# A transformer layer with sparse attention: first transfers reordered, two heads' compressed probabilities in one transpose, `p` split later

## The reference, cut to what matters

```
q, k_c, v_c, k_s, v_s, k_w, v_w, gate = split(rms_norm(x) @ w_in)
k_c, v_c = compress(k_c), compress(v_c)      # 15 blocks of 32 tokens, stride 16; silu(blk @ w1) @ w2
pc = masked_softmax(q @ k_c.T * scale)       # 15 columns: the compressed branch
ps = masked_softmax(q @ k_s.T * scale)       # all 256 tokens are selected here: causal
pw = masked_softmax(q @ k_w.T * scale)       # the window is 512: causal as well
o = gate0 * (pc @ v_c) + gate1 * (ps @ v_s) + gate2 * (pw @ v_w)
h = x + o @ w_out
```

## Time and profile before

| | us |
|---|---|
| median of three runs | 1208.03 (1207.96 to 1209.53) |
| profiled execution, own time | 1209.89 |
| its span | 1207.8 |
| TensorE busy | 1196.9 |
| VectorE busy | 729.1 |
| ScalarE busy | 590.7 |

### The profile page before, as it was taken

The page is one execution under the profiler, slowest core; times in us unless marked ns, Lnnn a source line. Parts: engine busy times, 40 slices in busy tenths (PEclk is TensorE's granted clock), DMA queues, the critical chain, the costliest instruction groups (busy, mean ns, idle before and its releaser), DMA issues.

```text
span 1207.8 us, 15258 instructions
## 1 busy us (share of the span) xinstructions
PE 1196.9 (99%) x5502; PEld 993.3 (82%) x5502; DVE 729.1 (60%) x956; ACT 590.7 (49%) x812; POOL 71.5 (6%) x63
## 2 busy tenths in 40 slices
PE   8999999999999999999999999999999999999998
PEld 7787788888888888888888888888888888888886
DVE  5676646777767647554465464555655457476554
ACT  6654444666656544443344443444433445455442
POOL 1000000000000002100011100011100012000000
PEclk9999999999999999999999999999999999999999
DMA  9776564333348766865567765577665676785661
GB/s 353 251 228 211 186 195 139 104 123 105 105 144 266 223 222 217 253 224 193 188 215 244 240 215 194 189 237 242 220 217 191 208 245 214 248 266 195 212 208 51
DMA packets 107134, 247.02 MB, mean 205 GB/s; under 512 B 9408, under 2 KB 52160, under 8 KB 107072
## 3 DMA queue, kind: packets, MB, share of 16 engines
q1 hardware_dynamic: 106784, 245.98, 62.4%
q10 hardware_dynamic: 288, 0.27, 0.1%
HBM read 232.58 MB, written 13.63 MB: 204 GB/s over the span
## 4 chain that ended last, share of the span: by engine, by line
PE 92%; DVE 3%; ACT 2%; DMA 2%; issue 1%; SPq 0%; ACTq 0%; DVEq 0%
PE acc L1413 85%; DMA w_raw<-in_nsa_w_in_units_dram 2%; PE sc L1554 2%; DVE w_split L936 1%; PE tr L1471 1%; ACT w_split L595 1%; ACT s L693 1%; PE sc L1519 0%; PE sc L1460 0%; PE tr L1460 0%; PE tr L1605 0%; PE tr L1606 0%; PE acc L1443 0%; ACT junk_act L645 0%; PE tr L1583 0%
## 5 line engine op out<-in xcount | busy, mean ns | idle before, releaser
L936 DVE TENSOR_TENSOR w_split<-w_raw,w_split 128x1024 fp32r<-128x1024 f32 x411 | 509.3, 1249 | 384.2 <-ACT w_split L595 383.7
L595 ACT ACTIVATE w_split<-w_raw 128x1024 fp32r<-128x1024 f32 x411 | 431.4, 1058 | 413.0 <-PE acc L1413 407.2
L1413 PE MATMUL acc<-w_split,a_hi 128*128 128x512 f32 x1916 | 595.5, 392 | 1.7 <-DVE w_split L936 1.7
L1413 PE MATMUL acc<-w_split,b_split 128*128 128x512 f32 x1920 | 441.0, 390 | 0.0
L1413 PEld LDWEIGHTS acc<-w_split,a_hi 128*128 128x128 f32 x1916 | 357.0, 188 | 77.0 <-DVE w_split L936 3.0
L1413 PEld LDWEIGHTS acc<-w_split,b_split 128*128 128x128 f32 x1920 | 359.3, 188 | 74.2
L1413 PE MATMUL acc<-w_split,a_lo 128*128 128x512 f32 x958 | 373.5, 390 | 0.0
L1413 PEld LDWEIGHTS acc<-w_split,a_lo 128*128 128x128 f32 x958 | 180.2, 188 | 38.0
L559 POOL TENSOR_TENSOR stage<-stage 128x512 f32<-128x512 f32 x32 | 49.8, 1577 | 558.8 <-ACT stage L603 558.8
L693 ACT ACTIVATE s<-s,nmx,q_scale 128x128 f32<-128x128 f32 (+1 forms) x64 | 34.2, 540 | 5.4 <-DVE nmx L1103 5.4
L603 ACT ACTIVATE stage<-acc,rstd 128x512 f32<-128x512 f32 x48 | 30.1, 678 | 11.3 <-PE acc L1413 8.2
(11 more groups left out here) (185 smaller groups left out, 516.3 us busy)
## 6 DMA issues: line engine op xcount, KB each, us to landing
w_raw<-in_mlp_w_units_dram SPq DMA_DIRECT2D x256, 512.0 KB, 4.3
w_raw<-in_nsa_w_in_units_dram SPq DMA_DIRECT2D x79, 512.0 KB, 4.3
w_raw<-in_nsa_w_out_units_dram SPq DMA_DIRECT2D x32, 512.0 KB, 3.8
w_raw<-in_ple_w_gate_units_dram SPq DMA_DIRECT2D x32, 512.0 KB, 3.6
turn_dram<-junk SPq DMA_DIRECT2D x44, 128.0 KB, 4.3
turn_dram<-s SPq DMA_DIRECT2D x44, 128.0 KB, 4.3
v_slc<-turn_dram SPq DMA_DIRECT2D x22, 256.0 KB, 4.4
v_win<-turn_dram SPq DMA_DIRECT2D x22, 256.0 KB, 4.2
```

Of the source, the lines that this page charges most:

```text
L595: nc.scalar.activation(w_hi[:, u % SPLIT], w_raw[:, u % RAW], ACT.Copy).then_inc(hi_done, 1)
L936: nc.vector.tensor_tensor(w_lo[:, u % SPLIT], w_raw[:, u % RAW], f32(w_hi[:, u % SPLIT]), ALU.subtract).then_inc(lo_done, 1)
L1413: last = nc.tensor.matmul(acc[c % 2][t][:], xs[:, kt, toks], ws[:, u % SPLIT, m * NW:(m + 1) * NW], start=(kt == 0 and n == 0), stop=(kt = ...
```

## The change

There are four groups of edits.

- **Start.** The first two slices of `x` move from ScalarE's DMA queue to SP's, one ahead of each half of the first weight unit, with a semaphore each (`first_x`); ACT and DVE split `x` slice 0, weight half 0, `x` slice 1, in this order. `keep_busy` runs 10 plain matmuls of zeros (the left half of `causal`, which GpSimd now clears first) instead of 18 transposes, and no longer waits for the identity.
- **Sums of `x`.** The squares of chunks 0 and 1 move to k = 6 and 7 of `C_KC`, those of 2 and 3 stay at k = 0 and 1 of `C_VC`, so that there is one chunk behind each unit. `mean_square` moves to k = 1, `to_stage(C_KC)` to k = 2.
- **Compressed probabilities.** `cmp_p` has 4 x 16 columns for each head, so that two heads fill 128. At an even head PE transposes both (two transposes of 128 columns), ACT copies 128 rows, DVE subtracts in rows 0 to 15 and 64 to 79. At an odd head none of it is done, and ACT's copy of `p_t` releases `tr[1]`. `v_cmp` is stored twice, in rows 0 to 47 for even and 64 to 111 for odd heads, the other rows zero; so its copy, its subtraction and `hidden_out(1)` are done twice.
- **`p`.** It gets room of its own under `p_t`, is loaded when the last head is done (SP waits for `o_done`), and split in `C_OUT + 3`, k = 0 and 1.

```diff
         kc_split = sb("kc_split", [P, G, 2, CSTEP], F32R)
-        v_cmp = sb("v_cmp", [P, NW], F32R)
...
+        with nc.sbuf_tensor("p_raw", [P, 2, SEQ], F32) as p_raw, \
+                nc.sbuf_tensor("pt_hi", [P, 2, SEQ], F32R) as pt_hi, nc.sbuf_tensor("pt_lo", [P, 2, SEQ], F32R) as pt_lo:
+            pass
...
-        cmp_p = sb("cmp_p", [P, 2, TT, HPG, 3, CSTEP])
+        cmp_p = sb("cmp_p", [P, 2, TT, HPG, 4, CSTEP])
...
-        hid_3 = s0[:, 0].rearrange("p b s -> p (b s)")[:, 0:3 * BLOCKS].rearrange("p (g c n) -> p g c n", c=3, n=CSTEP)
+        hid_pair = p_t[:].rearrange("p b s -> p (b s)")[:, 2 * NW:].rearrange("p (g h c n) -> p g h c n", g=G, h=2, c=4)
...
-        p_raw = s1[:, 0]
-        pt_hi = sb("pt_hi", [P, 2, SEQ], F32R)
-        pt_lo = sb("pt_lo", [P, 2, SEQ], F32R)
...
                         for m, full in enumerate((first_full, raw_full[0])):
+                            sp.dma_start(x_raw[:, m], x_cols[:, m]).then_inc(first_x[m], 16)
                             sp.dma_start(slot(0)[:, m], packed(w_in_units, col // NW, 0)[:, m]).then_inc(full, 16)
                         continue
                     if c == C_KC:
                         kts = slice(UNIT_KT * k, UNIT_KT * (k + 1))
-                        sp.dma_start(x_raw[:, kts], x_cols[:, kts]).then_inc(x_cols_full[k], 16)
+                        sp.dma_start(x_raw[:, kts], x_cols[:, kts]).then_inc(x_cols_full[k - 1], 16)
                     load(u, packed(w_in_units, col // NW, k), slot(u))
                     if c == C_KC and k >= 4:
...
                         sp.dma_start(cmp_w2[:], nsa_cmp_w2[0].rearrange("k d e -> d k e")).then_inc(cmp_w2_full, 16)
-                        sp.dma_start(p_raw, p_cols).then_inc(p_full, 16)
...
+                    elif k == UPC - 1:
+                        sp.wait_ge(o_done, H)
+                        sp.dma_start(p_raw[:], p_cols).then_inc(p_full, 16)
...
+            nc.gpsimd.memset(causal[:], 0.0).then_inc(busy_zeros, 1)
             nc.gpsimd.memset(ident[:], 0.0)
             nc.gpsimd.memset(fold[:], 0.0)
             nc.gpsimd.memset(f32(kc_split[:]), 0.0)
-            nc.gpsimd.memset(causal[:], 0.0)
...
-            nc.gpsimd.memset(s0[:, 0], 0.0)
+            nc.gpsimd.memset(hid_pair, 0.0)
...
-            act.dma_start(x_raw[:, 0:UNIT_KT], x_cols[:, 0:UNIT_KT]).then_inc(x_cols_full[0], 16)
...
-            def x_part(k):
-
-                act.wait_ge(x_cols_full[k], 16)
-                for kt in range(UNIT_KT * k, UNIT_KT * (k + 1)):
+            def x_part(k, kts=None):
+
+                if k:
+                    act.wait_ge(x_cols_full[k - 1], 16)
+                for kt in kts or range(UNIT_KT * k, UNIT_KT * (k + 1)):
+                    if not k:
+                        act.wait_ge(first_x[kt], 16)
                     nc.scalar.activation(a_hi[:, kt], x_raw[:, kt], ACT.Copy, scale=const_t[:, kt:kt + 1])\
...
-                nc.scalar.activation(p_t[:, hh % 2, NW:NW + SEQ], tr[1][:, 0:SEQ], ACT.Copy)
-                nc.scalar.activation(p_cmp[0:3 * CSTEP, hh % 2], tr[1][0:3 * CSTEP, SEQ:NW], ACT.Copy)\
-                  .then_inc(p_cmp_hi, 1)
+                last = nc.scalar.activation(p_t[:, hh % 2, NW:NW + SEQ], tr[1][:, 0:SEQ], ACT.Copy)
+                if hh % 2:
+                    last.then_inc(tr_done[1], 1)
+                else:
+                    nc.scalar.activation(p_cmp[:, hh // 2 % 2], tr[1][:, SEQ:NW], ACT.Copy).then_inc(p_cmp_hi, 1)
...
-            x_part(0)
+            x_part(0, (0,))
             act.wait_ge(first_full, 16)
             nc.scalar.activation(w_hi[:, 0, 0:NW], w_raw[:, 0, 0:NW], ACT.Copy).then_inc(first_hi, 1)
+            x_part(0, (1,))
+
+            def x_sums(n):
+                act.wait_ge(x_full[n], 16)
+                sum_squares(0, n)
+
             for k in split_hi(FIRST[C_KC], UPC):
                 if k < UPC - 1:
                     x_part(k + 1)
+                if k >= 6:
+                    x_sums(k - 6)
             for k in split_hi(FIRST[C_VC], UPC):
                 if k < 2:
-                    for n in range(2 * k, 2 * k + 2):
-                        act.wait_ge(x_full[n], 16)
-                        sum_squares(0, n)
-                if k == 3:
+                    x_sums(k + 2)
+                if k == 2:
                     act.wait_ge(const_full, 16)
                     act.wait_ge(rs_ready, 1)
                     to_stage(C_KC, rstd[:, 0])
...
-                    nc.scalar.activation(v_cmp[0:3 * CSTEP], sc[0][0:3 * CSTEP, :], ACT.Copy).then_inc(v_cmp_hi, 1)
-                if k == 6:
-                    act.wait_ge(p_full, 16)
-                    nc.scalar.activation(pt_hi[:], p_raw, ACT.Copy).then_inc(p_hi, 1)
+                    for half in range(2):
+                        rows = slice(half * P // 2, half * P // 2 + 3 * CSTEP)
+                        last = nc.scalar.activation(v_cmp[rows, half], sc[0][rows, :], ACT.Copy)
+                    last.then_inc(v_cmp_hi, 1)
...
                 if k == 2:
                     turned_gain(T_H1, a_hi, 0, GAIN_MLP)
+                if k == 0:
+                    act.wait_ge(p_full, 16)
+                    nc.scalar.activation(pt_hi[:], p_raw[:], ACT.Copy).then_inc(p_hi, 1)
...
-                    nc.vector.tensor_copy(hid_3[:, :, :, 0:N_CMP],
-                                          own[:, :, None, :].to_broadcast([P, G, 3, N_CMP])).then_inc(hid_copied, 1)
+                    for half in range(2):
+                        last = nc.vector.tensor_copy(hid_pair[:, :, half, 0:3, 0:N_CMP],
+                                                     own[:, :, None, :].to_broadcast([P, G, 3, N_CMP]))
+                    last.then_inc(hid_copied, 1)
...
-                nc.vector.tensor_tensor(cmp_p[:, g % 2].rearrange("p t j c n -> p (t j) c n")[:, :, :, 0:N_CMP],
+                nc.vector.tensor_tensor(cmp_p[:, g % 2].rearrange("p t j c n -> p (t j) c n")[:, :, 0:3, 0:N_CMP],
...
             def head_pt(hh):
-                dve.wait_ge(p_cmp_hi, hh + 1)
-                nc.vector.tensor_tensor(p_cmp[0:CSTEP, hh % 2], tr[1][0:CSTEP, SEQ:NW],
-                                        f32(p_cmp[0:CSTEP, hh % 2]), ALU.subtract).then_inc(tr_done[1], 1)
+                if hh % 2:
+                    return
+                dve.wait_ge(p_cmp_hi, hh // 2 + 1)
+                for half in range(2):
+                    rows, b = slice(half * P // 2, half * P // 2 + CSTEP), hh // 2 % 2
+                    last = nc.vector.tensor_tensor(p_cmp[rows, b], tr[1][rows, SEQ:NW], f32(p_cmp[rows, b]),
+                                                   ALU.subtract)
+                last.then_inc(tr_done[1], 1)
...
             dve.wait_ge(mix_full, 16)
-            x_part(0)
+            x_part(0, (0,))
             dve.wait_ge(first_hi, 1)
             nc.vector.tensor_tensor(w_lo[:, 0, 0:NW], w_raw[:, 0, 0:NW], f32(w_hi[:, 0, 0:NW]),
                                     ALU.subtract).then_inc(first_lo, 1)
+            x_part(0, (1,))
             for k in split_lo(FIRST[C_KC], UPC):
                 if k < UPC - 1:
                     x_part(k + 1)
             for k in split_lo(FIRST[C_VC], UPC):
+                if k == 1:
+                    mean_square(0, 0)
                 if k == 2:
-                    mean_square(0, 0)
-                if k == 3:
                     dve.wait_ge(rs_ready, 1)
                     nc.vector.tensor_scalar(neg_rstd[:], rstd[:, 0], -1.0, None, ALU.mult).then_inc(neg_ready, 1)
...
-                    nc.vector.tensor_tensor(v_cmp[2 * CSTEP:3 * CSTEP], sc[0][2 * CSTEP:3 * CSTEP, :],
-                                            f32(v_cmp[2 * CSTEP:3 * CSTEP]), ALU.subtract).then_inc(vc_ready, 1)
+                    for half in range(2):
+                        rows = slice(half * P // 2 + 2 * CSTEP, half * P // 2 + 3 * CSTEP)
+                        last = nc.vector.tensor_tensor(v_cmp[rows, half], sc[0][rows, :], f32(v_cmp[rows, half]),
+                                                       ALU.subtract)
+                    last.then_inc(vc_ready, 1)
...
-                if k == 6:
-                    dve.wait_ge(p_hi, 1)
-                    nc.vector.tensor_tensor(pt_lo[:], p_raw, f32(pt_hi[:]), ALU.subtract).then_inc(p_split, 1)
...
             for k in split_lo(FIRST[C_OUT + 3], UPC):
+                if k == 1:
+                    dve.wait_ge(p_hi, 1)
+                    nc.vector.tensor_tensor(pt_lo[:], p_raw[:], f32(pt_hi[:]), ALU.subtract).then_inc(p_split, 1)
...
-                    own = hid_3[:, g].rearrange("p c n -> p (c n)") if kv else hid[:, at:at + N_CMP]
-                    last = nc.tensor.matmul(bank[0:3 * CSTEP if kv else N_CMP, g * DK:(g + 1) * DK], own,
+                    own = hid_pair[:, g].rearrange("p h c n -> p (h c n)") if kv else hid[:, at:at + N_CMP]
+                    last = nc.tensor.matmul(bank[0:P if kv else N_CMP, g * DK:(g + 1) * DK], own,
...
```

(24 more changed lines are left out.)

## The result

| | median of its runs, us | lowest to highest | profiled execution, own time | its span |
|---|---|---|---|---|
| before | 1207.99 | 1207.85 to 1209.53 | 1209.89 | 1207.8 |
| after | 1214.78 | 1212.26 to 1216.11 | 1212.47 | 1210.4 |

The ratio is 1.0046, with an interval of [1.0036, 1.0057] (fast runs only): slower, and outside the range of 1203.6 to 1206.8. In the profiled pair the difference is 2.58 us. That execution is one of the two quickest of after, both with a mean granted clock of 0.998; the other four lie 2.2 to 3.6 us higher, with a mean of 0.995 to 0.997.

The account below looks back on a forecast made before the run. TensorE, busy 99% of the span, was taken as the bound. Gains of 1.77 + 1.1 + 0.69 + 0 = 3.56 us from 1208.03 gave 1204.5 us, range 1203.6 to 1206.8.

Parts of the forecast that it names:

- The step that failed: From 357 us to the end: TensorE has no wait, so all earlier gains stay; no loss sized.
- The start: First weight units: earlier first product, but second unit no earlier, landings unmoved; value 0, bounds +0.1 and -0.9 us.
- The expectation of the first product: Kernel start: TensorE's first product at about 5.7 us instead of 7.42.
- The rival with late loads: Start: landings move 0.9 us back with the issues, time 1205.4; chance 0.09, shared with costly wide transposes.
- The clock in the new gap: Start: clock falls in TensorE's idle after the first unit, line 0.9 us late, time 1205.4; chance 0.17.
- The transposes: Compressed probabilities: eight odd heads lose 16 transposes at 0.111 us each, wide ones cost no more; gain 1.77 us.
- The bound from the weight loads: Compressed probabilities: 128-wide transposes could cost up to 37 ns more each, 0.6 us in all, leaving a gain of 1.2.
- The sums: Squares of x: TensorE's waits near 36 and 55 us shrink or go; gains 1.1 and 0.69 us.
- One sign of being wrong: C_KC k = 7, expected ready at 28.05 against 28.26 us, would be late because of chunk 0.
- The stretch at 199 us: Half-clock stretch after tiny products, costing 1.7 us, taken as absent usually; rival that it stays: 1206.2, chance 0.15.
- The rival on the slow side: head_output of eight even heads: second subtraction stops TensorE beyond 1.43 us of delay; time 1210.5, chance 0.04.
- The sum: Whole kernel: terms add to 3.56 us, taken from the median 1208.03 to give 1204.5 us.

Follow-up runs that it names:

- a_pad14: The kernel after with 14 more identity transposes (28 instructions) behind its first half unit; 1205.62 us, ratio 0.9976.
- a_pad7: The kernel after with 7 more identity transposes (14 instructions) behind its first half unit; 1205.1 us, ratio 0.9974.
- a_pad4: The kernel after with 4 more identity transposes (8 instructions) behind its first half unit; 1205.12 us, ratio 0.9973.
- a_up228: The kernel after with 228 wait-only TensorE instructions spread over 16 units ahead of the MLP loop; 1206.12 us, ratio 0.998.
- b_cmp: The kernel before with only the compressed-probabilities and late-p edits, plus 32 wait-only instructions keeping the loop's place; 1206.58 us, ratio 0.9983.
- b_sums: The kernel before with only the new order of the sums of x; 1206.48 us, ratio 0.9986.
- a_oldstart: The kernel after with the start of the kernel before, plus 32 wait-only instructions keeping the loop's old place; 1204.0 us, ratio 0.9964.
- a_actx: The kernel after with 14 filler transposes and the first two x slices back on ScalarE's queue, one transfer each; 1205.83 us, ratio 0.9975.
- b_keep4: The kernel before with 4 instead of 18 idle transposes ahead of the first product, 28 instructions fewer; 1218.73 us, ratio 1.0076.

## Why the prediction was wrong, point by point

- **The step that failed**: "From 357 us on TensorE has no wait until the end, so what is gained before stays gained." The first half was read rightly off the trace of before. The second half took the end to be indifferent to edits far ahead of it. It was not: 28 instructions fewer in front of a loop moved it by part of a block, and its two jumps cost 9.2 us (1214.78 - 1205.62), of which 6.7 us are seen in the profiled execution as waits and half clock. The step counted the removed transposes' time and not their place in the program, and no rival held such a thing. Its own term, the cost of a jump, stood at nothing without a reason; it measured 2.24 and 2.78 us of waits and 1.7 us of clock. The DMA view of before had the hint: its instruction queue has no packet between 600 and 900 us, so the loop fitted; the same view of after has 14 there.
- **The start, sized 0 (bounds +0.1 and -0.9)**: it costs 1.1 to 1.6 us by medians whose intervals overlap. "The DMA engines are behind the issues by then, so the landings stay" failed: they move 137 GB/s in the first six us where it was 174, and the second unit is 1.3 us later. The step read the queue's fullness from a stretch at 20 us for a moment at which it was not full. The expectation of the first product (5.7 us) was near: 5.26. The rival with late loads (1205.4) names this and had its size.
- **The clock in the new gap**: the rival (0.17, 1205.4) came true in some executions. After idles of 2.80 and 2.22 us the profiles of after and `a_pad14` have full clock, and so has `a_pad7`. In `a_pad4` and `a_up228` there are 3.4 us at half clock behind the gap, from 13.05 and 12.15 us on. `a_pad4`:

```profile
12.14 0.70 PE L1442 MATMUL acc<-w_split,a_hi 128*128 128x512 f32 x2 [1.95 <-DVE w_split L954]
...
14.07 1.05 PE L1442 MATMUL acc<-w_split,a_hi 128*128 128x512 f32 x2
```

Its third unit starts at 16.56 us where that of `a_pad7` starts at 14.86, 1.7 us later; at 67 us 0.84 us are left of it, as the rival had it (0.9). It is not the cause of 1214.8: `a_pad4` and `a_pad7` both have 1205.1. The length of the idle doesn't tell when the clock falls (no fall behind 2.80 us in after, one behind 1.95 us here), and the prediction's "the drop at 199 us agrees" rests on an idle of 0.44 us.
- **The transposes, 1.77 us**: right. 0.112 us each at an even head, 0.67 us at an odd one; `b_cmp` is 1.8 us below before. The bound from the weight loads (37 ns each, and more by the rule of the Trainium skill, page "TensorE: Matmul & The Clock Gate", section LDWEIGHTS) did not come true: the wide ones load in 140 ns and keep the same pitch.
- **The sums, 1.1 + 0.69 us**: right in kind, and in size by the medians; `b_sums` gives 1.8 us with an interval of 0.6 to 2.8. In after itself the first part went into the start (level at 44.4 us), and the second is seen at 55.35. One sign of being wrong did come: k = 7 of `C_KC` is late, by a wait of 0.26 us in after and of 0.84 in `a_pad14`; neither `a_oldstart` nor `b_sums` has it, so the new start is needed for it.
- **The stretch at 199 us**: a toss. It is absent in the profiles of after, `a_pad14`, `a_pad7`, `a_actx`, `b_cmp` and `a_up228`, and there in before and in those of the other six runs.
- **The rival on the slow side** (the second subtraction): the product waits for nothing it can be seen to wait for, but the room shrank from 1.43 to 0.18 us. That edit cost nothing with little to spare.
- **The sum**: the forecast of 1204.5 is near what the change gives with its start undone and its loop in place, 1204.0, and that is in part luck, since that kernel's profile has the first products at full clock. With the start it is 1205.1 to 1205.6. The rest is the jumps.

## What to carry to other kernels

When an edit takes instructions from or adds them to an engine that runs a long loop later, look at the instruction queue: packets in the page, and whether any fall into the loop's later turns. If the count rises, shift the loop by a few instructions of filler in a place where the engine idles anyway, before judging the edit; here 8 instructions made 9.7 us. Look in the profile whether it does idle there: in `a_actx` the same filler held the engine up by 1.7 us. A change that loses time far behind its own place has moved something other than work. And at a start, read the transfer rate of the very microseconds in which new issues go ahead of old ones, not that of the steady stretch.

## What the runs showed that was not expected

- A loop of 1620 instructions on TensorE runs again without a fetch or is fetched anew each turn, by its place to within 8 instructions. The waits are 2.2 to 3.8 us per jump when the loop starts 1 to 8 instructions before a block's end by the reckoning above, and 0.5 us or nothing when it starts 29 or more before it.
- A stall of 2.2 us or more can be followed by a stretch at half clock: 3.4 us of it behind the first jump of after and of `b_keep4`, 6.8 us behind the second of `b_keep4`, none behind the second of after (2.78 us idle). With the mean clocks (0.995 to 0.998 in after, 0.998 to 1.0 in `a_pad14`) this fits that the runs of after scatter over 3.9 us and those of `a_pad14` over 1.3.
- 120 wait-only instructions, on a semaphore long past, cost TensorE nothing that can be measured (1208.41 against 1208.31 us).
